# Differential exponentials drawn once: maps made in the joint stage, scaled on VectorE, added on GpSimd, and kept in DRAM

## What is computed

```
s = einsum('bqmhd,bkmhd->bmhqk', q, k) * DH_A ** -0.5
s = where(dist >= 0, s - slopes * dist, NEG_INF)
p = softmax(s, axis=-1)
p = p[:, 0] - lam * p[:, 1]
o = einsum('bhqk,bkhd->bqhd', p, v)
```

## Time and profile before

| | us |
|---|---|
| median of 3 runs (2540.29 to 2546.51) | 2545.97 |
| profiled execution, span | 2554.0 |
| of it projections and all before the joint stage | 941 |
| joint stage (first gate product to first score of attention A) | 471 |
| attention A | 264 |
| attention B | 344 |
| sampled rows, then merge | 155 + 379 |

### The profile page before, as it was taken

The page is one execution under the profiler, slowest core; times in us unless marked ns, Lnnn a source line. Parts: engine busy times, 40 slices in busy tenths (PEclk is TensorE's granted clock), DMA queues, the critical chain, the costliest instruction groups (busy, mean ns, idle before and its releaser), DMA issues. The chain is left out here.

```text
span 2554.0 us, 34275 instructions
## 1 busy us (share of the span) xinstructions
PE 2459.9 (96%) x12691; PEld 1965.0 (77%) x12691; DVE 1572.7 (62%) x2540; ACT 910.6 (36%) x1449; POOL 186.4 (7%) x182
## 2 busy tenths in 40 slices
PE   5999999999999999999999999999999897999998
PEld 2788888887788878888888778877777654788886
DVE  3411336644676417778886788977877656655564
ACT  3211122225333228884001556644444433222221
POOL 0000112210232100000000200000000000000000
PEclk9999999999999999999999899999999998999999
DMA  8653645555455477764445866446466397545541
GB/s 305 231 192 146 226 133 165 165 167 203 139 159 141 143 228 195 200 162 126 146 144 142 178 150 149 96 82 133 93 137 156 116 320 269 170 144 149 144 141 55
DMA packets 296286, 417.51 MB, mean 163 GB/s; under 512 B 62624, under 2 KB 180136, under 8 KB 286581
## 3 DMA queue, kind: packets, MB, share of 16 engines
q1 hardware_dynamic: 283630, 382.18, 52.6%
q10 hardware_dynamic: 11456, 33.30, 3.5%
q0 software_dynamic: 1056, 0.13, 0.1%
HBM read 277.88 MB, written 137.65 MB: 163 GB/s over the span
## 5 line engine op out<-in xcount | busy, mean ns | idle before, releaser
L1884 DVE CUSTOM_DVE_ANT_0 max_s_ps<-max_s_ps,max_causal 128x128 f32<-128x128 f32 (+7 forms) x256 | 194.3, 769 | 70.0 <-PE max_s_ps L1942 50.8
L704 PE MATMUL proj_z<-first_km,h_hi 128*128 128x512 f32 x576 | 230.1, 399 | 3.2 <-DVE first_v L1276 3.2
L704 PE MATMUL proj_z<-first_km,h_lo 128*128 128x512 f32 x576 | 226.1, 393 | 0.0
L704 PE MATMUL proj_z<-first_v,h_hi 128*128 128x512 f32 x576 | 224.4, 390 | 0.0
L2267 ACT ACTIVATE att_b_pf<-att_b_s_ps 128x1024 f32<-128x1024 f32 (+2 forms) x160 | 142.4, 898 | 102.9 <-PE att_b_s_ps L2310 79.6
L1843 ACT ACTIVATE max_s_ps<-max_s_ps,max_neg_top 128x128 f32<-128x128 f32 (+2 forms) x192 | 161.2, 840 | 43.2 <-DVE max_neg_top L1884 31.6
L2284 DVE TENSOR_TENSOR att_b_p_lo<-att_b_pf,att_b_p_hi 128x1024 fp32r<-128x1024 f32 (+2 forms) x160 | 170.5, 1066 | 5.5
L1887 DVE TENSOR_REDUCE max_neg_top<-max_s_ps 128x1 f32<-128x1024 f32 x128 | 154.2, 1225 | 17.9 <-PE max_s_ps L1942 11.4
L2279 DVE CAST att_b_p_hi<-att_b_pf 128x1024 fp32r<-128x1024 f32 (+2 forms) x160 | 98.1, 613 | 70.0 <-ACT att_b_pf L2267 67.4
L1051 POOL TENSOR_TENSOR proj_rstd<-proj_rstd,keep_neg_half 128x8 f32<-128x8 f32 (+1 forms) x68 | 112.7, 1658 | 323.8 <-DVE proj_rstd L1374 323.8
L1242 ACT ACTIVATE proj_work<-proj_z 128x512 f32<-128x512 f32 x64 | 38.3, 598 | 270.3 <-PE proj_z L704 270.3
(11 more groups left out here) (475 smaller groups left out, 6148.2 us busy)
## 6 DMA issues: line engine op xcount, KB each, us to landing
w_raw<-in_w_in SPq DMA_DIRECT2D x144, 256.0 KB, 3.7
smp_v_a<-scratch_mixes SPq DMA_DIRECT2D x16, 1024.0 KB, 5.2
map_qm<-scratch_q_hi SPq DMA_DIRECT2D x48, 256.0 KB
map_k<-scratch_k_hi SPq DMA_DIRECT2D x37, 256.0 KB
head_w<-in_w_ada SPq DMA_DIRECT2D x8, 1024.0 KB, 6.8
scratch_mixes<-proj_out SPq DMA_DIRECT2D x32, 256.0 KB, 3.1
scratch_k_hi<-proj_work SPq DMA_DIRECT2D x32, 256.0 KB, 2.3
scratch_k_lo<-proj_work SPq DMA_DIRECT2D x32, 256.0 KB, 2.8
```

The source lines that it names most:

```text
L704: ins = nc.tensor.matmul(out, left(*lt), right(*rt), start=first and n == 0, stop=last and n == len(terms) - 1)
L1884: nc.vector.tensor_tensor_reduce(s, s, causal[:, 1024 - w:1024], -1.0, -NEG, ALU.add, ALU.min, accum_out=neg_top[:, kh, u, qt:qt + 1]).the ...
```

## The change

The exponentials of the differential maps are taken once, in the joint stage, and kept.

- **Joint stage** (`gates_and_maps`). The eight forgetting units come first, the differential maps after them, now row tile by row tile: `rows` lists 64 (head, row tile) pairs, in each head tiles 0 to 7 and then 15 down to 8. A row has the two maps m, and for tiles 8 to 15 ("late rows") two parts kh each: 0 is 1024 keys wide, 1 is the diagonal part of 128 to 1024. A late row is four tasks, an early row two. The diagonal part's maximum takes that of part 0 as its start, and the exponentials of a map wait for its last maximum; they go to SBUF, `p0` (a ring of 5) and `p1` (a ring of 3), with their row sums.
- One row later VectorE computes from the sums 1/sum0 (kept as `scale_a`) and factor = -lam * sum0/sum1 (`factors`: a reciprocal and a product, and for late rows a sum of the parts ahead of them), and multiplies `p1` by the factor. **GpSimd** adds it to `p0`. SP stores `p0` to `maps` in DRAM (float32, keys along the row). The 96 parts of a core's maps are 69,632 columns, 36 MB.
- The gate weights' buffers are smaller: a front half with two places and a back half with one. Gate tiles are made in halves, 96 pieces of 12 matmuls. Only forgetting units still have shifts to store. ScalarE issues the gate tiles' stores.
- **Attention A** loads the maps in blocks of 512 queries by 512 keys (40 blocks, 8 places; the 16 diagonal blocks in four parts of growing width). PE transposes them, 128 x 128 at a time (544), ScalarE's copy makes the high part straight from PSUM, VectorE subtracts for the low part, and PE makes the three products with V as before, now for one step at a time. The output is multiplied by `scale_a`. SP also loads attention B's first two heads during this stage. V's high part of head 0 is asked for at the joint stage's end.
- Some buffers live shorter or elsewhere; the projection's stage no longer computes and stores a shifted bias (`bias_c`, `bias_col`).

```diff
 def gates_and_maps(k):
+    in_chunk = [(0, 0), (1, 0), (0, 1), (1, 1)] + [(j, half) for j in range(2, T - 2) for half in range(2)]
+    in_chunk += [(T - 2, 1), (T - 1, 1), (T - 2, 0), (T - 1, 0)]
+    rows = [(h, qt) for h in range(HA) for qt in MAP_ROWS]
+    a_tasks = [("a", g, qt, m, kh) for g, (h, qt) in enumerate(rows) for m in range(2) for kh in range(qt // 8 + 1)]
...
-        due.append(int((at - spent) / PRODUCT))
+        due.append(min(int((at - spent) / PRODUCT), (NP - TAIL) * EACH))
...
             @block.gpsimd
+                for g, (h, qt) in enumerate(rows):
+                    for kh in range(qt // 8 + 1):
...
+                        first = p0[:, seg % P0_RING, 0:w]
+                        pool.wait_ge(scaled, seg + 1)
+                        nc.gpsimd.tensor_tensor(first, first, p1[:, seg % P1_RING, 0:w], ALU.add).then_inc(comb_done, 1)
...
             @block.sync
+                def store_map(g):
...
+                        sp.wait_ge(comb_done, seg + 1)
+                        sp.dma_start(k.maps[h][qt * P:qt * P + P, kh * 1024:kh * 1024 + w],
+                                     p0[:, seg % P0_RING, 0:w]).then_inc(k.map_stored[seg % P0_RING], 16)
...
+                weights_due(NP * EACH)
+                store_map(len(rows) - 1)
+                sp.wait_ge(z_done, TURNED * T)
+                load_v(k, sp, 0, HI)
...
             @block.scalar
+                def probabilities(x):
...
+                    act.wait_ge(max_done, last_of(g, m) + 1)
...
+                    nc.scalar.activation(dst, scores(x), ACT.Exp, bias=neg_top[:, g % 4, m, both:both + 1],
+                                         scale=-1.0 if kh == qt // 8 else 1.0, accum_out=total).then_inc(exp_done, 1)
...
             @block.vector
+                def combine(g, kh):
...
+                    second = p1[:, seg % P1_RING, 0:w]
+                    step.wait(dve)
+                    nc.vector.tensor_scalar(second, second, factor[:, g % 4:g % 4 + 1], None, ALU.mult).then_inc(scaled, 1)
...
             @block.tensor
+                def free(x):
+                    y = earlier[x]
+                    if y >= 0 and tasks[y][0] == "a":
+                        pe.wait_ge(exp_done, order[y] + 1)
...
 def attention_a(k):
+                map_pieces_stored(k, sp)
...
+                for b, (h, g, kg) in enumerate(blocks):
+                    if b >= PIECES:
...
+                        sp.wait_ge(t_done, 4 * (b - PIECES) + 4)
+                    load_block(b)
+                    if b == 1:
+                        load_v(k, sp, 0, LO)
+                    if b == 3:
+                        for part in (HI, LO):
+                            load_v(k, sp, 1, part)
+                    if b == PIECES:
                         load_b(k, sp, 0)
+                    if b == PIECES + 6:
+                        load_b(k, sp, 1)
...
-                    nc.scalar.activation(pf[:, n // 2 % PR, :, at:at + w], s_ps[:, n % PLACES, :, 0:w], ACT.Exp,
-                                         bias=a.bias[h % 2][:, col:col + 1]).then_inc(p_done, 1)
+                    nc.scalar.activation(p_hi[:, n % HR, 0:w], turned[:, n % PLACES, 0:w], ACT.Copy).then_inc(hi_done, 1)
...
-                    nc.vector.scalar_tensor_tensor(pc[:, m % CR, 0:w], pf[:, m % PR, 1, 0:w], k.neg_lam[:], pf[:, m % PR, 0, 0:w],
-                                                   ALU.mult, ALU.add).then_inc(diff_done, 1)
```

928 lines of the change are left out of this document (497 added, 431 removed).

## The result

The changed kernel takes 2647.03 us (median of 4 runs, 2645.24 to 2648.57) against 2546.24 us: a ratio of 1.0394, 95% interval 1.0378 to 1.041. Slower was forecast; 2564 us, and even the range's upper end of 2618, were far too low. The profiled execution has a span of 2646.8 us, 92.8 more than before, where 18 were forecast.

The account below looks back on a forecast made before the run. TensorE was taken to bound the joint stage and attention A. The joint stage 82 us longer, attention A 64 us shorter: 18 us on the 2554.0 us span, 2572, less 8 for the median: 2564 us, range 2518 to 2618.

Parts of the forecast that it names:

- Part 1: Joint stage, attention B's scores with 614 gate products: 208 us of TensorE, so differential scores start at 1149.
- Part 2: Joint stage, differential rows with 490 gate products: TensorE 197 us, rows' chain 173 us, taken as 205 us, ending at 1354.
- TensorE idle before 1350: Sign named in advance that the joint stage's price for the rows' chain was wrong.
- Part 3: Joint stage, last 22 rows without gate products: 104 us by the chain plus 9 for the clock, last reduction at 1469.
- Nearer the second row: Clock cost in the last 22 rows, 9 us between none and 20, leaning to a profile row at clock 0.94.
- GpSimd's addition: Joint stage: 2.3 us per 1024 columns, 156 us for 96 additions beside 320 us, hidden at either end except the last.
- The first rival: Joint stage: GpSimd and VectorE exclude each other, late rows' scalings wait for additions, 35 us, 2592 us; chance 0.24.
- The seam and attention A: From last reduction to attention B: first map piece asked for at +9, attention B at +227 instead of +291, 64 us earlier.
- DMA becomes the bound: Attention A: the queue needs 213 us for maps, V and attention B's loads, more than TensorE's 156 us.
- The second rival: Attention A: DMA is not the bound, attention B at +183, 44 us less, 2520 us; chance 0.22.
- the fourth: Joint stage stays as long as it was, all of A's work fitting beside the products: 2482 us; chance 0.04.
- The third rival: Attention A: TensorE drops to half clock throughout, 312 us from +20, 2676 us; chance 0.04.

Follow-up runs that it names:

- e13: Changed kernel with VectorE combining alone, six and two map buffers, K loads and gate products spread over rows, map stores issued by ScalarE: 2563.1 us.
- e3: Changed kernel with the 15 K loads at each head change spread over rows 0, 3 and 5 on SyncE's queue: 2629.6 us.
- e5: Changed kernel with the 96 map stores issued by ScalarE, one row late, instead of SyncE: 2628.3 us.
- e10: Changed kernel with 56 of the 64 rows left out of each K load of heads 1 to 3 in the joint stage: 2623.5 us.
- e15: e13 without the spreading of gate products, so the last 22 rows have none again: 2588.7 us.
- e1: Changed kernel without GpSimd's addition, VectorE combining the maps alone: 2632.7 us.
- e16: Changed kernel, GpSimd adding, with both scalings before a row's first addition, K loads and gate products spread, map stores issued by ScalarE: 2600.3 us.
- e18: e13 with five and three map buffers instead of six and two: 2576.5 us.
- e2: Changed kernel with both scalings of a row put ahead of its first GpSimd addition: 2644.4 us.
- e19: e16 with the scalings interleaved with the additions again, as in the changed kernel: 2600.9 us.
- e9: Changed kernel with 112 of 128 partitions left out of the loads of 18 whole map blocks in attention A: 2640.3 us.
- e17: Changed kernel with four output buffers in attention A instead of two: 2642.2 us.
- e14: e13 with four output buffers in attention A and its loads of V and attention B's operands reordered on the queue: 2556.4 us.

## Why the prediction was wrong, step by step

**Part 1, attention B's scores first: right.** 208 us were forecast for it, up to 1149. The first score of a differential map starts at 1157.4 and its exponential at 1159.0, with TensorE 99% busy up to there; 5 of the 10 us come from the later start of the first gate product, which was left at no change.

**Part 2, the rows with gate products: this step failed.** "As both bind at times, I take 197 + 8 = 205 us" weighed TensorE and the rows' chain, and no term stood for SyncE's queue. It was left at nothing, although the change puts 96 map stores that wait for other engines into the same queue as the loads of keys, queries and weights. The last gate product beside a row starts at 1413.8 instead of 1354:

```profile
1413.82 0.40 PE L2124 MATMUL max_z<-h_hi,first_v 128*128 128x512 f32 x1
```

Two head changes (11 and 14 us over the same rows of e13) and the two rows at the weight loads (9 and 11) are 45 of these 60 us, 10 more come from the start at 1159 instead of 1149. "TensorE idle before 1350" was the sign named for a wrong chain; it came, but from the queue. e3 and e5 show it by moving only what stands in this queue, and e10 by thinning it. With the third head change below, the queue and its transfers are 55 of the 83 us by which the forecast of 2564 was missed.

**Part 3, the rows without products: mechanism right, size off.** 135 us instead of 115. 10 are the third head change, again the queue. The late rows were put at 6.0 us each and 9 us for the clock; 13 of them take 7.2 us in the mean. In e13, with products beside them and a clock of 1.00, they take 6.4, and 7.2 again in e15, without products. From this an estimate for 14 rows is 6 us that the chain was priced too low, and 11 us or more for the clock instead of 9. "Nearer the second row" was a wrong reading, though it hardly moved the sum: the rows stood at 0.5 to 0.6, and the row at 0.94 has unbroken products up to 2153.7 and then waits of 1.7 and 4.3 us, not short ones.

**GpSimd's addition: right in size, wrong in what it costs.** 2.3 us were taken for 1024 columns and 2.34 to 2.41 came, 166.6 us in all against 156. "Hidden at either end" did not hold: e1 puts 14 us on the addition with its lock, and e16 against e18 24 us. That it holds a buffer of the ring longer fits both, but was not tested by itself.

**The first rival, the lock: its mechanism came, its price did not.** It was priced at 28 us. The trace has it in the late rows, and the second scaling does start inside the addition as worked out. The evidence taken against it, an instruction of 8 columns, was as weak as the text feared. The Trainium skill, SBUF — State Buffer, Who interferes with whom, says that whichever of the two starts first has the shared ports for its whole instruction; by that rule the trace agrees, 2.19 us instead of 0.55. e1 takes it away together with the addition for 14 us, and e2 and e19 remove and restore it at no change of time, each against an addition that starts later or earlier. So 28 us was probably too much, and the lock's own price is not shown.

**The seam and attention A: the sum right, one reason wrong.** 225 us against 227. "DMA becomes the bound" holds for the first 130 us only (share 1.02 to 1.09); from 1700 on TensorE is 97% busy and the share 0.67. TensorE's 156 us were 175 busy from 1570 to 1775, at a mean clock of 0.90, and some 40 us were waits, of TensorE from 1549 to 1775:

```profile
PE att_a_turned L2272 <- DMA att_a_maps<-scratch_maps: 21.2, 3, 11.7
...
PE att_a_acc L2299 <- DVE att_a_p_lo L2256: 13.0, 2, 10.7
...
PE att_a_acc L2292 <- DMA first_v<-scratch_v_lo: 4.9, 1, 4.9
```

The second goes back to an output store. So one bound handed over to the other, and the sum came near by luck; e9 shows it, since a stage bound by DMA throughout would have given back 30 us or more. What each of the waits costs alone stays open: e17 and e14 moved them more than they removed them. The second rival's 183 us for the seam and attention A did not come, and the fourth's unchanged joint stage neither (603 us instead of 446). The third rival, half clock all through attention A, did not come: 1700 to 1775 has 1.00 with four transposes to three products. The Trainium skill, TensorE: Matmul & The Clock Gate, PE-mode transpose, says that transposes do not count as busy for the clock in the same way; by that rule the row neither agrees nor disagrees, since no stretch of attention A has transposes alone.

**The sum itself.** e13, whose rows no queue holds, starts its last exponential at 1472.4 and ends at 2563.1 us, where the prediction had 1469 and 2564. The agreement is partly luck, as e13 combines on VectorE, has a sixth buffer and spreads its products. e15, with the products where the change put them, ends at 2588.7 us. So with nearly no waits on the queue and VectorE alone, the change comes within 25 us of the forecast; the same with GpSimd adding and the products unspread was not run.

## What to carry to other kernels

When a change makes results leave the core in a stage that had only loads, write down the issuing queue as an engine of its own: every issue by its time, in order, with the waits that stand between, at the places where loads come in bursts. A ring of buffers emptied through such a queue should outlast its longest burst plus the slowest landing; here one buffer more was worth 13 us. Help from a second engine can cost more than it saves although its busy time is hidden, here 14 to 24 us: price the path of a piece through it too.
